# Where split weights begin in on-chip memory, modulo 256 bytes, in a two-block transformer kernel

## The chip, the cores and the metric

One core of a Trainium2 chip. The metric is the device time of one launch, in microseconds (us), the median of several runs. All arithmetic is fp32 to the reader; large products are made of three single-pass products of fp32r operands (below).

## The reference

Two transformer blocks, 256 tokens, width 1024. The first has two layers and carries a context of another 256 tokens beside the tokens, so that its first layer works on 512 columns; its last layer needs of the context only keys and values, and works on 256.

```python
for layer in range(2):
    h_ctx = modulate(rms_norm(ctx, norm_mix[layer]), c_shift1, c_scale1)
    qc, kc, vc, hyc, gc = split(h_ctx @ w_in[layer])        # the last layer: kc, vc only
    h = modulate(rms_norm(x, norm_mix[layer]), shift1, scale1)
    q, k, v, hy, g = split(h @ w_in[layer])
    attn, hyo = latent_attention(q, k, v, kc, vc), hyena_mix(hy, ...)
    merged = g_attn * (attn @ w_o_attn) + g_hyena * (hyo @ w_o_hyena)
    x = x + gate1 * (merged @ w_out[layer])                 # the context likewise, not in the last layer
    x = x + gate2 * swiglu(modulate(...), w_gate_up[layer], w_down[layer])
# second block: a mixer (convolution and dilated attention), memory attention, 32 experts
x = x + mixed(x @ w_in_2) @ w_out_2
x = x + memory_cross_attention(h, m, w_xq, w_xk, w_xv, w_xo)
x = x + hierarchical_moe(h, ...)                            # 32 experts of 1024 x 512, top 2
return rms_norm_2(x, final_norm_g)
```

## The kernel before

**Layout.** Activations lie with the channel on the 128 partitions and tokens along the free axis: tile k of 8 is `[128, tokens]`. A weight matrix is cut into blocks of 128 x 128; eight blocks make a unit of 1024 columns, 4096 bytes in each partition (`UF = 1024`, `UB = 8`). The units come from HBM in one long order (`stream_order`), each with one DMA of 512 KB on SyncE's queue (line 2842), into a ring of `NS = 6` places. A DMA into a place waits until TensorE has used the unit that lay there (`stream.spent`). After the last unit SyncE goes on with the experts' weights (line 2890): 192 transfers of 1024 KB into 15 slots, three of which are the ring and one the high places; the first of them stands right behind the last unit of the ring in SyncE's queue.

**Split weights.** Every streamed weight is split: ScalarE copies the unit, rounded to fp32r, into one of `NHI = 3` high places (`ac_split`, line 431), and VectorE subtracts that from the unit and leaves the low part in the ring place itself (`ve_split`, line 439). Activations are held as a high and a low part too (HH and H, or parts of `area`, KF, VT, YF, KX, VX, tmp). A product is then three: high weight by high activation, high by low, low by high.

**Direct and turned products.** In a direct product the weight block is stationary (it is loaded into the array) and the activations move: `pe_block` (line 460, nearly all), `pe_pair` (line 475), `pe_down` (line 1608) and line 2104. In a turned product 128 tokens are stationary and the weights move: the values of `w_in` (line 927, 256 columns), the values of `w_in_2` (line 1833, 256 columns) and `w_xv_2` (line 1974, 512 columns). The first layer's direct products move 512 columns, and so do the two key blocks of the second layer; all other direct products move 256. TensorE's instructions are in a fixed order; a matmul is preceded by the load of its stationary operand, which runs beside the matmul before it.

**Addresses.** Tiles are allocated one after the other from the address behind a scratch region of 16384 bytes (the default of the builder) and 128 bytes of constants: X begins at 16512, which is 128 modulo 256. X, H, HH, area, KX, VX, VT, YF, KF have sizes that are multiples of 256 bytes, and so all begin at 128 modulo 256; every block within them is a multiple of 512 bytes further on. `con` begins there too; behind it come smaller tiles, tmp and PPT begin at 32 modulo 256. The ring begins at 192064, that is 64 modulo 256, and its places are 4096 bytes apart; the high places begin at 216640, 64 modulo 256 as well. The last of them ends at 228928, and the partition has 229376 bytes.

Lines that the prediction names: 431 and 439 (the splits), 460, 475, 1608 (direct products), 927, 1833, 1974 (turned products), 701 and 709 (the modulation's multiplies and sums, on tiles of the same shape as a unit), 2842 and 2890 (SyncE's transfers).

Of the kernel before, what the change touches and what calls it, by code (L numbers as in the profile page):

```python
# [16 lines left out]
P = 128  # L17
EPS = 1e-6
LN_EPS = 1e-5
UB = 8  # L20
EB = 16
UF, EF = UB * P, EB * P
NS = 6
NHI = 3
# [101 lines left out]
class Signal:  # L126
# [4 lines left out]
    def __init__(self, sem):  # L131
        self.sem, self.n, self.value = sem, 0, {}
# [79 lines left out]
class Stream:  # L212


    def __init__(self, units, slots, sems, ub):
        self.units, self.slots, self.sems, self.ub = units, slots, sems, ub
        self.where = {u: i for i, u in enumerate(units)}
        self.spent = {}

    def slot(self, i):  # L220
        return self.slots[i % len(self.slots)]
# [9 lines left out]

STREAM2 = [("w_xk_2", 0, 6), ("w_in_2", 0, 22), ("w_xv_2", 0, 8), ("w_xk_2", 6, 7), ("w_out_2", 0, 8), ("w_xk_2", 7, 8),
# [8 lines left out]
def stream_order():  # L241
    units = []
    for l in range(2):
        units += [("w_in", l, u) for u in range(24)]
        for j in range(8):
            units += [("w_in", l, 24 + 2 * j), ("w_in", l, 25 + 2 * j), ("w_o_attn", l, j)]
            if j % 2 == 0:
                units.append(("w_o_hyena", l, j // 2))
        for name, n in (("w_out", 8), ("w_gate_up", 44), ("w_down", 22)):
            units += [(name, l, u) for u in range(n)]  # L250
    for name, u0, u1 in STREAM2:
        units += [(name, 0, u) for u in range(u0, u1)]
    return units

# [13 lines left out]
def two_blocks_kernel(nc, T):  # L268
    ctx = ExitStack()
    with ctx:  # L270
# [8 lines left out]
        N = 256  # L279
        X = sb("X", 4096)[:, :].rearrange("p (k t) -> p k t", k=8)  # L280
# [38 lines left out]
        ring, ringr = sb2("ring", NS * UF)  # L319
        his_flat, his = sb2("his", NHI * UF)  # L320
# [48 lines left out]

        def sem(name):  # L370
            return ctx.enter_context(nc.semaphore(name))
# [29 lines left out]
        stream = Stream(stream_order(), [ring[:, i * UF:(i + 1) * UF] for i in range(NS)], [sem(f"s_w{i}") for i in range(NS)], UB)  # L401
# [6 lines left out]
        eslots += [ring[:, i * EF:(i + 1) * EF] for i in range(NS // 2)]  # L408
# [7 lines left out]
        def hi_slot(n):  # L416
            return his[:, (n % NHI) * UF:(n % NHI + 1) * UF]

        def lo_slot(i):
            r = i % NS  # L420
            return ringr[:, r * UF:(r + 1) * UF]
# [451 lines left out]
        pos = {b: n for n, b in enumerate(W_IN_ORDER)}  # L873
# [2163 lines left out]
```

## Time and profile before

| | |
|---|---|
| median of 3 runs | 2082.8 us (2080.1, 2082.8, 2088.5) |
| the profiled execution, first to last instruction | 2084.6 us |
| TensorE matmul / weight load busy | 91% / 75% |
| VectorE / ScalarE / GpSimd busy | 55% / 43% / 1% |
| mean granted TensorE clock | 0.967 of full |

The profiled execution has no time of its own besides its span; the span lies inside the three runs. A clock of 1.00 in a row is 2.4 GHz, 0.50 is 1.2 GHz. Durations of matmuls overlap, since they are pipelined: the pace of a run of matmuls is the distance from start to start, not the duration of one. From 1575 us on the kernel streams the experts' weights at about 420 GB/s to its end.

### The profile page before, as it was taken

The page shows a single profiled execution, that of the slowest core. Times are in us where ns is not written, and L with a number is a line of the kernel's source. Part 1 is how long each engine was busy: PE and PEld are TensorE (multiplying, and loading weights), DVE is VectorE, ACT ScalarE, POOL GpSimd, SP SyncE. Part 2 cuts the span into 40 slices and gives each one's busy share as a digit, 9 for nine tenths or more (in the row PEclk, how much of TensorE's full clock was granted, in tenths as well). Part 3 has the DMA queues.
Part 4 walks back from the last instruction along what each step waited for, and adds up shares of the span by engine and source line. Part 5 has one row for each costly group of instructions (what it writes and reads, how often), then busy time and mean ns, then how long its engine had stood idle before and what let it go on. Part 6 is the DMA issues. An engine that isn't in the chain of part 4 may idle for free.

```text
span 2084.6 us, 33760 instructions
## 1 busy us (share of the span) xinstructions
PE 1889.2 (91%) x14150; PEld 1554.0 (75%) x14150; DVE 1156.6 (55%) x1898; ACT 903.5 (43%) x1532; POOL 16.9 (1%) x31
## 2 busy tenths in 40 slices
PE   7999989999999999999899999999999767776666
PEld 4877668888778888798699999997898544454344
DVE  3555757776887788567656667689755111111012
ACT  4333345665756677455445555634844000000001
POOL 0000000000000000000000000000000000000000
PEclk8999999999999999999999999999999998999987
DMA  8222024553555555234055555543247999999995
GB/s 319 85 71 81 1 76 158 183 179 105 180 179 177 188 193 170 91 102 142 11 182 192 182 183 184 173 162 112 90 144 325 420 420 420 419 419 420 420 421 236
DMA packets 91121, 428.01 MB, mean 205 GB/s; under 512 B 11089, under 2 KB 12754, under 8 KB 66002
## 3 DMA queue, kind: packets, MB, share of 16 engines
q1 hardware_dynamic: 78866, 382.51, 49.3%
q10 hardware_dynamic: 12096, 43.26, 6.2%
q8 instruction: 114, 1.87, 0.4%
q14 instruction: 45, 0.37, 0.1%
HBM read 424.68 MB, written 1.05 MB: 204 GB/s over the span
## 4 chain that ended last, share of the span: by engine, by line
PE 64%; DMA 20%; DVE 8%; ACT 5%; issue 2%; SPq 1%; ACTq 0%; POOL 0%; DVEq 0%; POOLq 0%
PE bank L460 41%; PE bank L1608 8%; DMA area<-in_w 8%; DMA his<-in_w 4%; DMA ring<-in_w 4%; DMA PPT<-in_w 3%; PE bank L475 2%; PE bank L2497 2%; PE bank L2453 1%; DVE st L1259 1%; PE bank L1187 1%; PE bank L2104 1%; PE bank L927 1%; ACT PPT L1204 1%; DVE ring_r L439 1%
## 5 line engine op out<-in xcount | busy, mean ns | idle before, releaser
L439 DVE TENSOR_TENSOR ring_r<-ring,his_r 128x1024 fp32r<-128x1024 f32 x314 | 383.5, 1223 | 226.9 <-ACT his_r L431 225.5
L460 PE MATMUL bank<-HH_r,his_r 128*128 128x256 f32 (+1 forms) x1504 | 499.1, 332 | 1.4 <-DVE ring_r L439 1.4
L460 PE MATMUL bank<-HH_r,ring_r 128*128 128x256 f32 (+1 forms) x1504 | 492.2, 327 | 0.0
L460 PE MATMUL bank<-H_r,his_r 128*128 128x256 f32 (+1 forms) x1440 | 472.8, 328 | 0.0
L431 ACT ACTIVATE his_r<-ring 128x1024 fp32r<-128x1024 f32 x314 | 330.6, 1055 | 303.5 <-PE bank L460 273.4
L460 PEld LDWEIGHTS bank<-HH_r,his_r 128*128 128x128 f32 x1504 | 284.1, 189 | 35.2 <-issue 8.6
L460 PEld LDWEIGHTS bank<-HH_r,ring_r 128*128 128x128 f32 x1504 | 283.7, 189 | 25.1
L460 PEld LDWEIGHTS bank<-H_r,his_r 128*128 128x128 f32 x1440 | 270.7, 188 | 27.0 <-issue 1.0
L2469 DVE TENSOR_TENSOR tmp<-tmp,bank 128x128 f32<-128x128 f32 x64 | 18.4, 288 | 385.9 <-ACT tmp L2462 262.7
L460 PE MATMUL bank<-area_r,his_r 128*128 128x256 f32 (+1 forms) x480 | 148.8, 322 | 0.0
L2453 PE MATMUL bank<-area,KF 128*32 128x128 f32 x1888 | 86.1, 312 | 44.3 <-DMA area<-in_w 39.3
L1608 PE MATMUL bank<-VT_r,ring_r 128*128 128x512 f32 (+1 forms) x352 | 118.6, 337 | 0.0
L1608 PE MATMUL bank<-YF_r,his_r 128*128 128x512 f32 (+1 forms) x352 | 118.1, 336 | 0.0
L1608 PE MATMUL bank<-VT_r,his_r 128*128 128x512 f32 (+1 forms) x352 | 117.5, 334 | 0.0
L2453 PEld LDWEIGHTS bank<-area,KF 128*32 128x32 f32 x1888 | 70.6, 125 | 58.2 <-DMA area<-in_w 49.9
L460 PEld LDWEIGHTS bank<-area_r,his_r 128*128 128x128 f32 x480 | 90.1, 190 | 7.4
L2508 ACT ACTIVATE H<-bank 128x512 f32<-128x512 f32 x16 | 9.6, 597 | 191.3 <-PE bank L2497 191.3
L709 ACT ACTIVATE rst<-rst 128x1024 f32<-128x1024 f32 x80 | 83.6, 1045 | 1.6 <-DVE rst L701 1.6
L2497 PE MATMUL bank<-area,tmp 128*32 128x512 f32 x256 | 56.9, 646 | 20.1 <-DMA area<-in_w 19.5
L1335 ACT ACTIVATE VT_r<-area 128x512 fp32r<-128x512 f32 (+1 forms) x96 | 49.9, 523 | 51.0 <-PE bank L1608 45.3
L1608 PEld LDWEIGHTS bank<-YF_r,his_r 128*128 128x128 f32 x352 | 66.1, 188 | 7.7
L1608 PEld LDWEIGHTS bank<-VT_r,his_r 128*128 128x128 f32 x352 | 65.9, 187 | 7.6 <-DVE YF_r L1339 0.2
(415 smaller groups left out, 3301.0 us busy)
## 6 DMA issues: line engine op xcount, KB each, us to landing
area<-in_w SPq DMA_DIRECT2D x91, 1024.0 KB, 27.3
ring<-in_w_in SPq DMA_DIRECT2D x102, 512.0 KB, 3.5
ring<-in_w_gate_up SPq DMA_DIRECT2D x88, 512.0 KB, 3.5
ring<-in_w SPq DMA_DIRECT2D x36, 1024.0 KB, 27.4
HH<-in_w SPq DMA_DIRECT2D x26, 1024.0 KB, 26.8
ring<-in_w_down SPq DMA_DIRECT2D x44, 512.0 KB, 3.5
KX<-in_w_mod_rows ACTq DMA_DIRECT2D x28, 512.0 KB, 3.5
VX<-in_w_mod_rows ACTq DMA_DIRECT2D x28, 512.0 KB, 3.5
```

The source lines that it names most:

```text
L431: ac.eng.activation(hi_slot(n), stream.slot(u), ACT.Copy).then_inc(*ac_hi.up(n))
L439: ve.eng.tensor_tensor(lo_slot(u), stream.slot(u), hi_slot(n).bitcast(F32), ALU.subtract).then_inc(*ve_lo.up(n))
L460: ins = pe.eng.matmul(out, a, b, start=k == 0 and m == 0, stop=end)
L475: ins = pe.eng.matmul(out, a, b, start=k + m == 0, stop=k == 7 and m == 2)
L709: ac.eng.activation(prod, prod, ACT.Copy, accum_out=MODS[l][:, j, s:s + 1]).then_inc(*ac_mod.up("sum", n, s))
L927: ins = pe.eng.matmul(vb[tb // 2][:, o:o + 256], x[:, k, sl], w, start=k == 0 and n == 0 and o == 0, stop=k == 7 and n == 2 and o > 0)
L1187: ins = pe.eng.matmul(out[:, 0:256], vs(kc), c.pts[g % 2][:, kc * 256:(kc + 1) * 256], start=kc == 0, stop=kc == c.nk - 1)
L1204: ac.eng.activation(p[:, m * w:(m + 1) * w], src[:, m * w:(m + 1) * w], ACT.Exp, bias=st[:, so + m:so + m + 1], scale=c.rq(h, i + m) if c. ...
L1335: ac.eng.activation(hi, src, ACT.Copy).then_inc(*ac_cut.up(*key))
L1608: ins = pe.eng.matmul(banks.ap("ff", l, 4 * half + n)[:, 0:t], w, x, start=k == 0 and i == 0, stop=k == 21 and i == 2)
L2453: ins = pe.eng.matmul(out[32 * n:32 * n + 32, 0:P], HG[g % 2][:, k, 32 * j:32 * j + 32], w, start=k == 0, stop=k == 7, tile_position=(0, 3 ...
L2497: ins = pe.eng.matmul(out[32 * j:32 * j + 32, :], AT[j][:, 32 * k:32 * k + 32], w, start=k == 0, stop=k == 3, tile_position=(0, 32 * j))
```

## The change

Each streamed unit gets a lead, the number of floats by which it begins behind the start of its ring place and of its high place. Places become 64 floats (256 bytes) wider, `UW = UF + 64`. The lead is 0 (`BEHIND_512`), 16 (64 bytes, `BEHIND_256`) or 48 (192 bytes, `BEHIND_TURNED`), by the width of the products that read the unit. The class: the first block's layer 0, the two key units of its layer 1 and `w_xv_2` are 0; the value units of `w_in` and `w_in_2` are 48; everything else is 16. A small tile `level` in front of the ring brings the ring, and with it the high places, to the residue modulo 256 at which X begins. The scratch region is set to 8192 bytes, which makes room. The order of units, of instructions and of waits is the same, and so are all sizes that are moved or computed.

```diff
--- before.py
+++ after.py
@@ -212,13 +212,14 @@
 class Stream:
 
 
-    def __init__(self, units, slots, sems, ub):
+    def __init__(self, units, slots, sems, ub, leads=None):
         self.units, self.slots, self.sems, self.ub = units, slots, sems, ub
+        self.leads = leads or [0] * len(units)
         self.where = {u: i for i, u in enumerate(units)}
         self.spent = {}
 
     def slot(self, i):
-        return self.slots[i % len(self.slots)]
+        return self.slots[i % len(self.slots)][:, self.leads[i]:self.leads[i] + self.ub * P]
 
     def arrived(self, i):
         return self.sems[i % len(self.slots)], 16 * (i // len(self.slots) + 1)
@@ -229,6 +230,9 @@
 
 
 
+FIRST_BLOCK = ("w_in", "w_o_attn", "w_o_hyena", "w_out", "w_gate_up", "w_down")
+UW = UF + 64
+BEHIND_512, BEHIND_256, BEHIND_TURNED = 0, 16, 48
 STREAM2 = [("w_xk_2", 0, 6), ("w_in_2", 0, 22), ("w_xv_2", 0, 8), ("w_xk_2", 6, 7), ("w_out_2", 0, 8), ("w_xk_2", 7, 8),
            ("w_xq_2", 0, 8), ("w_xo_2", 0, 8)]
 
@@ -253,6 +257,18 @@
     return units
 
 
+def stream_leads(units, values):
+    leads = []
+    for name, l, u in units:
+        if name == "w_in" and u in values or name == "w_in_2" and 16 <= u < 22:
+            leads.append(BEHIND_TURNED)
+        elif name in FIRST_BLOCK and l == 0 or name == "w_in" and u < 2 or name == "w_xv_2":
+            leads.append(BEHIND_512)
+        else:
+            leads.append(BEHIND_256)
+    return leads
+
+
 def expert_order():
     units = []
     for g in range(8):
@@ -277,6 +293,7 @@
             return t, nc.alloc_sbuf_tensor_at(name + "_r", [P, cols], F32R, offset=at)
 
         N = 256
+        level = nc.sbuf_base
         X = sb("X", 4096)[:, :].rearrange("p (k t) -> p k t", k=8)
         H, HL = (t[:, :].rearrange("p (k t) -> p k t", k=8) for t in sb2("H", 4096))
         hh_flat, HH = sb2("HH", 4096)
@@ -316,8 +333,9 @@
         PP = [PPS[:, 512 * i:512 * i + 512] for i in range(2)]
         st = sb("st", 64)
         epsc = sb("epsc", 2)
-        ring, ringr = sb2("ring", NS * UF)
-        his_flat, his = sb2("his", NHI * UF)
+        sb("level", (level - nc.sbuf_base) % 256 // 4)
+        ring, ringr = sb2("ring", NS * UW)
+        his_flat, his = sb2("his", NHI * UW)
         psum = [ctx.enter_context(nc.psum_tensor(f"bank{i}", [P, 512], F32)) for i in range(8)]
 
 
@@ -367,6 +385,8 @@
         SG = [KX[:, 0, 256 * i:256 * i + 256].rearrange("p (b s) -> p b s", b=2) for i in range(2)]
         SGT = [VX[:, i, :] for i in range(2)]
 
+        pos = {b: n for n, b in enumerate(W_IN_ORDER)}
+
         def sem(name):
             return ctx.enter_context(nc.semaphore(name))
 
@@ -398,14 +418,15 @@
             return vec[0:rows, VEC[key] + i:VEC[key] + i + n]
 
         ident = cc("ident")
-        stream = Stream(stream_order(), [ring[:, i * UF:(i + 1) * UF] for i in range(NS)], [sem(f"s_w{i}") for i in range(NS)], UB)
+        stream = Stream(stream_order(), [ring[:, i * UW:(i + 1) * UW] for i in range(NS)], [sem(f"s_w{i}") for i in range(NS)], UB,
+                        stream_leads(stream_order(), [pos[b] for b in (10, 11)]))
         where = stream.where
 
         first = Stream([("w_mod", 0, u) for u in range(16)], [area[:, i * UF:(i + 1) * UF] for i in range(11)] +
                        [hh_flat[:, i * UF:(i + 1) * UF] for i in range(4)] + [KX_flat[:, :]], [sem(f"s_m{i}") for i in range(16)], UB)
         eslots = [con[:, 256:256 + EF]] + [area[:, i * EF:(i + 1) * EF] for i in (1, 2, 3, 0, 6, 4, 5)]
         eslots += [PPT[:, :], hh_flat[:, 0:EF], hh_flat[:, EF:2 * EF], his_flat[:, 0:EF]]
-        eslots += [ring[:, i * EF:(i + 1) * EF] for i in range(NS // 2)]
+        eslots += [ring[:, 2 * i * UW:2 * i * UW + EF] for i in range(NS // 2)]
         experts = Stream(expert_order(), eslots, [sem(f"s_e{i}") for i in range(len(eslots))], EB)
         over = Stream([(name, e, u) for e in range(32) for name, u in OVER_ORDER], [rsts_flat[:, :]], [sem("f_w")], UB)
         s_out = sem("s_out")
@@ -414,11 +435,12 @@
         nth = {i: n for n, i in enumerate(cut_units)}
 
         def hi_slot(n):
-            return his[:, (n % NHI) * UF:(n % NHI + 1) * UF]
+            at = n % NHI * UW + stream.leads[cut_units[n]]
+            return his[:, at:at + UF]
 
         def lo_slot(i):
-            r = i % NS
-            return ringr[:, r * UF:(r + 1) * UF]
+            at = i % NS * UW + stream.leads[i]
+            return ringr[:, at:at + UF]
 
 
         def ac_split(ac, upto):
@@ -870,7 +892,6 @@
 
 
 
-        pos = {b: n for n, b in enumerate(W_IN_ORDER)}
 
         def tokens(l):
             return 256 if l else 512
@@ -3026,7 +3047,7 @@
         arrays[name] = tiles(I[name][0], ub=EB)
     arrays["w2_2"] = rows_outermost(I["w2_2"][0])
 
-    nc = _bacc.Bacc("TRN2", target_bir_lowering=False, num_devices=1)
+    nc = _bacc.Bacc("TRN2", target_bir_lowering=False, num_devices=1, dynamic_dma_scratch_size=8192)
     T = {n: nc.dram_tensor("in_" + n, a.shape, mybir.dt.from_np(a.dtype), kind="ExternalInput").ap() for n, a in arrays.items()}
     T["out"] = nc.dram_tensor("out_0", (P, 8, 256), F32, kind="ExternalOutput").ap()
     T["deep"] = ("w_in", "w_gate_up", "w_mod", "w_mod_rows", "w_o_attn", "w_o_hyena", "w_out", "w_down", "w1_2", "w3_2", "w2_2")
```

## Rows read from the trace of the kernel before

**Rows 1.** The page: busy TensorE, and the chain's shares by engine and line

```profile
PE 1889.2 (91%) x14150; PEld 1554.0 (75%) x14150; DVE 1156.6 (55%) x1898; ACT 903.5 (43%) x1532; POOL 16.9 (1%) x31
...
PE 64%; DMA 20%; DVE 8%; ACT 5%; issue 2%; SPq 1%; ACTq 0%; POOL 0%; DVEq 0%; POOLq 0%
PE bank L460 41%; PE bank L1608 8%; DMA area<-in_w 8%; DMA his<-in_w 4%; DMA ring<-in_w 4%; DMA PPT<-in_w 3%; PE bank L475 2%; PE bank L2497 2%; PE bank L2453 1%; DVE st L1259 1%; PE bank L1187 1%; PE bank L2104 1%; PE bank L927 1%; ACT PPT L1204 1%; DVE ring_r L439 1%
```

**Rows 2.** Chain in order of time: start us, us, engine, tile, line, count

```profile
626.04 131.85 PE bank L460 x576
...
901.47 11.00 PE bank L927 x96
...
1150.08 68.08 PE bank L460 x576
...
1270.38 56.80 PE bank L1608 x480
...
1411.58 5.67 PE bank L1833 x48
...
1465.16 2.80 PE bank L1974 x12
```

**Rows 3.** Windows of TensorE: from:to, length, busy (count), clock, DMA share, GB/s

```profile
120.20:122.20 2.00, 2.00 (x6) 0.50 0.05 16
1341.00:1345.00 4.00, 4.00 (x23) 0.55 0.00 0
53.00:62.00 9.00, 9.00 (x82) 1.00 0.27 95
640.00:740.00 100.00, 100.00 (x439) 1.00 0.57 189
1160.00:1210.00 50.00, 50.00 (x427) 1.00 0.57 189
```

**Rows 4.** Timeline at half clock: start us, us, engine, line, tiles, array, columns

```profile
120.09 0.63 PE L460 MATMUL bank<-H_r,his_r 128*128 128x512 f32 x1
...
121.79 0.63 PE L460 MATMUL bank<-HH_r,ring_r 128*128 128x512 f32 x1
...
1340.61 0.41 PE L460 MATMUL bank<-HH_r,ring_r 128*128 128x256 f32 x1
...
1341.89 0.41 PE L460 MATMUL bank<-HH_r,ring_r 128*128 128x256 f32 x1
```

**Rows 5.** Groups by line: count | busy us, mean ns | idle before, releaser

```profile
L439 DVE TENSOR_TENSOR ring_r<-ring,his_r 128x1024 fp32r<-128x1024 f32 x314 | 383.5, 1223 | 226.9 <-ACT his_r L431 225.5
L701 DVE TENSOR_TENSOR rst<-KX,PPT 128x1024 f32<-128x1024 f32 x28 | 34.1, 1219 | 0.0
L431 ACT ACTIVATE his_r<-ring 128x1024 fp32r<-128x1024 f32 x314 | 330.6, 1055 | 303.5 <-PE bank L460 273.4 <-PE bank L2104 8.2 <-PE bank L927 7.3
L709 ACT ACTIVATE KX<-KX 128x1024 f32<-128x1024 f32 x28 | 29.3, 1046 | 0.0
```

**Rows 6.** The page: GB/s by slice, DMA queues, issues with KB and us to landing

```profile
GB/s 319 85 71 81 1 76 158 183 179 105 180 179 177 188 193 170 91 102 142 11 182 192 182 183 184 173 162 112 90 144 325 420 420 420 419 419 420 420 421 236
...
q1 hardware_dynamic: 78866, 382.51, 49.3%
q10 hardware_dynamic: 12096, 43.26, 6.2%
q8 instruction: 114, 1.87, 0.4%
...
area<-in_w SPq DMA_DIRECT2D x91, 1024.0 KB, 27.3
...
ring<-in_w SPq DMA_DIRECT2D x36, 1024.0 KB, 27.4
```

**Rows 7.** Timeline of SyncE's queue where the experts' transfers begin

```profile
1572.21 3.15 SPq L2842 DMA_DIRECT2D ring<-in_w_xo  x2
1575.41 0.43 SPq L2890 DMA_DIRECT2D con<-in_w  x1
```

## The prediction

> **What bounds the kernel now.** I read the page first: TensorE is busy 91% of the span, and the chain that ended last lies on it for 64%; line 460 alone carries 41% of the span, lines 1608 and 475 another 8% and 2% [rows 1]. All three are the same thing: a product of split weights (high by high, high by low, low by high), in single-pass fp32r. Next I read that chain in order of time, for its long unbroken runs. They show the pace: with 512 columns moving, 131.85 us for 576 products is 228.9 ns each; with 256 columns, 68.08 for 576 is 118.2 and 56.80 for 480 is 118.3 [rows 2]. The windows view sharpens it: a stretch holds (its length plus one product's duration) divided by the pace. So 100.00 us with 439 products of 0.39 us is 228.7 ns, and 50.00 us with 427 of 0.28 us is 117.7 [rows 3]. I use 228.9 and 117.7. In these stretches the granted clock is 1.00, TensorE never idles, and no wait ends late. What would make such a stretch shorter is a faster product, nothing else.
>
> How fast could it be? Where the granted clock was 0.50 (1.2 GHz), the same products start 4 intervals in 1.70 us (425 ns, 512 columns) and 6 intervals in 1.28 us (213 ns, 256 columns) [rows 3, 4]: the columns and nothing beside them. At 2.4 GHz that would be 213 and 107 ns. So at full clock a product loses 16 ns with 512 columns and 11 ns with 256, though no engine waits. The rows don't name the cause. The one thing that runs beside a product is the load of the next stationary operand, and both read the same partitions of on-chip memory.
>
> One pair of groups speaks for a matter of addresses. Line 927 has the operands turned round (256 columns of weights move, activations are stationary): 82 products of 0.28 us touch 9.00 us, or 113.2 ns [rows 3], and 96 with their slow start take 11.00 us (114.6) [rows 2]. Same columns, same fp32r, same clock, 4.5 ns less. What I vary in thought is the distance modulo 256 bytes from where the running product's moving operand begins to where the next stationary operand begins. By the order of allocation activations begin at 128 and ring and high places at 64. So direct products have distance 192, turned ones 64. But line 1833, turned as well and with distance 64, needs 118.1 (5.67 us for 48) [rows 2]: the same distance shows both paces.
>
> **The change, part by part.** No instruction, semaphore wait or DMA is added, removed or reordered on any queue; addresses alone move. The ring moves to residue 128 by 64 bytes of padding, each place is 256 bytes wider, and a unit begins 0, 64 or 192 bytes into it.
>
> (1) *Direct products, 256 columns.* Distance 192 becomes 64. Their count, from the streams: layer 1 has 36 + 8 + 4 + 8 + 44 + 22 = 122 units, the second block 48, each 24 products, 4080 in all. The nearest rows are line 927's 113.2 (a gain of 4.5 ns) and line 1833's 118.1 (no gain). I take 113.2: it held over 192 products in two layers, in long runs like those of the direct products, where line 1833 is broken up by waits. The last 144 products (6 units) come after the expert transfers have begun, which is the part where nothing is gained (below): 3936 x 4.5 = 17.7 us.
>
> (2) *Direct products, 512 columns.* Distance 192 becomes 0, which no fp32r row here has. Count: 124 units of layer 0 and the two key units of layer 1, x 24 = 3024. Bounds: 213 ns below (a gain of 16); above, the worst pace of any relation here, line 1974's 233.3 (2.80 us for 12, distance 64) [rows 2], a loss of 4.4. Between ends so far apart I go by the 256-column case: there the better placement keeps (113.2 - 106.5) / (117.7 - 106.5) = 0.6 of the loss. The same share of 16 ns is 9.5, so 222.5 ns, a gain of 6.4: 3024 x 6.4 = 19.4 us. This is the weakest term.
>
> (3) *Turned products.* Lines 927 and 1833 keep distance 64: nothing. Line 1974 (96 products) goes from 64 to 0: at most 0.02 us each, inside attention where VectorE sets the end. Nothing.
>
> (4) *The splits.* ScalarE and VectorE read and write ring and high places at one common residue before and after. VectorE's split takes 1223 ns, and a multiply of the same shape whose operands lie at other residues 1219; ScalarE 1055 against 1046 [rows 5]. Bounds +-4 and +-9 ns on 314 units. They are hidden: a unit lasts 24 x 118 = 2.8 us on TensorE against 1.22 on VectorE. If products drop to 113 it lasts 2.7, still covered. Zero.
>
> (5) *DMA.* A ring place is written from residues 128, 192 or 64 instead of 64. In the transfer-bound tail a megabyte lands in 27.4 us in the ring (residue 64) and 27.3 in the area (128) [rows 6]. Zero. The scratch cut from 16 to 8 KB pays for the 2304 wider bytes; its users would be GpSimd's transfers, and the queues shown are the two hardware ones and instruction fetch [rows 6]. Zero.
>
> **From the sum to the span.** Not every product is on the chain. Lines 460, 1608 and 475 make 51.4% of 2084.6 us there, 1071 us; their products at the paces above come to 3024 x 0.2289 + (4080 - 192) x 0.1177 = 1150 us (192 are line 2104's). Share 0.93. So (17.7 + 19.4) x 0.93 = 34.5 us. The tail: the first expert transfer is issued at 1575.41, right behind the last ring units (their wait is for TensorE to free a place) [rows 7]; from there 192 MB-sized transfers (201 MB) at the 420 GB/s of the page [rows 6] need 479 us, and TensorE waits for them. The tail keeps its length and moves forward with its start. What is late next is again a product: no new wait arises. The profiled span of 2084.6 lies inside the three runs (median 2082.8), so I subtract from the median: 2048 us.
>
> **The rule against it.** Rows first: at full clock a product costs 228.9 and 117.7 ns, 16 and 11 above its columns, and 113.2 at line 927 [rows 2, 3]. The Trainium skill, page SBUF — State Buffer, section "Who interferes with whom", says that TensorE has two independent read ports, one for the moving and one for the stationary operand, and never waits on anyone. By that the placement is worth nothing and the sum is 2083, rival 3. The difference between line 927 and line 460 is what the rule doesn't explain. The page TensorE: Matmul & The Clock Gate, section "Back-to-back issue gap", gives N / 2.4 + 2.5 ns, 215.8 for 512 columns; by it, an estimate, rival 1 ends near 2029 instead of 2022.
>
> **Rivals.**
> 1. *Free of loss at 512.* The 0 distance removes all 16 ns: 3024 x 15.9 = 48, with (1) 65.8 x 0.93 = 61, 2022 us. For: nothing but the cold rows. Against: the best pair at 256 kept 60% of its loss.
> 2. *One width gains alone.* Direct products settle as line 1833 does, or distance 0 is no better than 192: 17.7 x 0.93 = 16 or 19.4 x 0.93 = 18 us, 2065 to 2066. For: line 1833 has the new distance and the old pace.
> 3. *It doesn't do what it says.* The loss hangs on the order of reads, the output bank or the start of a run, not on residues; 927's gain is its four alternating outputs. 2083 us. For: 927 and 1833.
> 4. *Slower.* Distance 0 makes load and stream meet more often; 512 columns run at line 1974's 233.3 and 256 gains nothing: 3024 x 4.4 x 0.93 = +12, 2095 us. For: with 512 columns distance 64 is worse than 192, and 0 lies between the two. With (1) in full it decides only from 235 ns up.
>
> **How the numbers follow.** Chances: forecast (512 between 218 and 227 ns, 256 near 113) 0.45; rival 1 0.12; rival 2 0.20; rival 3 0.14; rival 4 0.09. The forecast's own range: 512 at 218 to 227 gives 2035 to 2061. The full range must take in rivals 2 and 3 to reach 8 in 10: 2030 to 2084; it leaves out rival 4 and most of rival 1. A measurement of this kernel can tell about 0.5%, 10.4 us, from no change. Faster by more (below 2072.4): 0.45 + 0.12 + 0.20 = 0.77; within: 0.14; slower: 0.09.
>
> **What would show it.** After: 576 products at line 460 with 512 columns in about 128 us of chain instead of 131.85, 576 with 256 columns in about 65.3 instead of 68.08; line 927 still 11.00 and line 1833 5.67; split durations unchanged; first expert transfer near 1541 instead of 1575.41, tail 489 us as now. Wrong if the 512 runs hold over 227 ns, if 256 columns run at 118, or if a wait for VectorE's low parts grows beyond a few us.

## The result, and the profile after

| | before | after |
|---|---|---|
| time, median of 4 runs each | 2082.9 us | 2071.5 us |
| ratio, 95% interval | | 0.9934, 0.9919 to 0.9949 |
| profiled execution: span | 2084.6 us | 2069.7 us |
| TensorE busy | 1889.2 us | 1880.4 us |
| first expert transfer issued at | 1575.4 us | 1562.4 us |

The change makes the kernel 0.66% faster, 13.7 us by the ratio (11.4 between the medians). The forecast was 34.5 us: right in sign, too large by a factor of 2.5. 2071.5 lies inside the full range (2030 to 2084), but outside the 2035 to 2061 that the forecast's own mechanism was given. A second set of runs gave 0.9934 again (0.9920 to 0.9947).

The page of the changed kernel: busy TensorE, and the chain's shares. Line numbers have moved: 460 is now 482, 1608 is 1629, 927 is 948, 1833 is 1854, 1974 is 1995, 439 and 431 are 461 and 453, 2890 is 2911.

```profile
PE 1880.4 (91%) x14150; PEld 1547.8 (75%) x14150; DVE 1155.6 (56%) x1898; ACT 903.6 (44%) x1532; POOL 17.0 (1%) x31
...
PE bank L482 42%; DMA area<-in_w 8%; PE bank L1629 8%; DMA his<-in_w 4%; DMA ring<-in_w 4%; DMA PPT<-in_w 3%; PE bank L497 2%; PE bank L2518 2%; PE bank L2474 1%; DVE st L1280 1%; PE bank L1208 1%; ACT PPT L1225 1%; PE bank L948 1%; DVE ring_r L461 1%; PE bank L2125 1%
```

The bound is what it was [rows 1]: TensorE on the products of split weights. The chain in order of time, to hold against [rows 2] (start us, us, engine, tile, line, count):

```profile
52.91 11.41 PE bank L948 x96
...
625.01 130.57 PE bank L482 x576
...
897.96 11.01 PE bank L948 x96
...
938.33 34.05 PE bank L482 x288
...
1144.28 65.29 PE bank L482 x576
...
1399.68 5.67 PE bank L1854 x48
```

576 products of 512 columns take 130.57 us for 131.85, or 226.7 ns each for 228.9. 576 of 256 columns take 65.29 for 68.08, or 113.3 for 118.2. But 288 products of 256 columns, the same line and the same distance, take 34.05 us, 118.2 each: they gained nothing. The turned products of line 948 take 11.41 us in layer 0 and 11.01 in layer 1, those of line 1854 5.67 as before. Line 927 had taken 11.00 in both layers. The windows say the same, against [rows 3]: 442 products in 100 us for 439, 445 in 50 us for 427.

```profile
640.00:740.00 100.00, 100.00 (x442) 1.00 0.59 195
1160.00:1210.00 50.00, 50.00 (x445) 1.00 0.58 194
```

The splits and the transfers are unmoved, against [rows 5] and [rows 6]; SyncE's queue reaches the experts 13.0 us earlier, against [rows 7]:

```profile
L461 DVE TENSOR_TENSOR ring_r<-ring,his_r 128x1024 fp32r<-128x1024 f32 x314 | 383.3, 1223 | 220.9 <-ACT his_r L453 219.6
L453 ACT ACTIVATE his_r<-ring 128x1024 fp32r<-128x1024 f32 x314 | 330.8, 1056 | 292.8 <-PE bank L482 262.6 <-PE bank L2125 7.9 <-PE bank L948 7.5
...
area<-in_w SPq DMA_DIRECT2D x91, 1024.0 KB, 27.5
...
ring<-in_w SPq DMA_DIRECT2D x36, 1024.0 KB, 27.3
...
1562.44 0.43 SPq L2911 DMA_DIRECT2D con<-in_w  x1
```

### The profile page after: what moved, and what is told of

Same layout as the page of the kernel before. It is cut to its first block, busy times and chain, and to the rows that moved or that the text cites. A ratio compares the mean times of both kernels' runs of the same rounds, so it can differ in the third digit from the quotient of the medians.

```text
span 2069.7 us, 33760 instructions
## 1 busy us (share of the span) xinstructions
PE 1880.4 (91%) x14150; PEld 1547.8 (75%) x14150; DVE 1155.6 (56%) x1898; ACT 903.6 (44%) x1532; POOL 17.0 (1%) x31
## 4 chain that ended last, share of the span: by engine, by line
PE 65%; DMA 19%; DVE 8%; ACT 5%; issue 2%; SPq 1%; ACTq 0%; DVEq 0%
PE bank L482 42%; DMA area<-in_w 8%; PE bank L1629 8%; DMA his<-in_w 4%; DMA ring<-in_w 4%; DMA PPT<-in_w 3%; PE bank L497 2%; PE bank L2518 2%; PE bank L2474 1%; DVE st L1280 1%; PE bank L1208 1%; ACT PPT L1225 1%; PE bank L948 1%; DVE ring_r L461 1%; PE bank L2125 1%
## 5 line engine op out<-in xcount | busy, mean ns | idle before, releaser
L1629 PEld LDWEIGHTS bank<-VT_r,ring_r 128*128 128x128 f32 x352 | 66.1, 188 | 6.9
```

The source lines that it names most:

```text
L1629: ins = pe.eng.matmul(banks.ap("ff", l, 4 * half + n)[:, 0:t], w, x, start=k == 0 and i == 0, stop=k == 21 and i == 2)
```

## How the runs are compared

In what follows "distance" is as in the prediction: start of the next stationary operand less start of the running moving operand, modulo 256 bytes. "Pace" is the mean interval from the start of one direct product to the start of the next, from all records of a trace; intervals over 240 ns (512 columns) or 124 ns (256), which hold a wait or are the slow first ones of a run, are left out. "Settled" means the mean of the last intervals of a piece, once they repeat. A "lead" is in floats of 4 bytes. "By pace" is 3024 times the change of the first pace plus 4080 times that of the second. All kernels on this table compute the reference in full.

| kernel | distances 512 / 256 | pace 512 | pace 256 | by pace | ratio to before (95%) | as us |
|---|---|---|---|---|---|---|
| before | 192 / 192 | 229.06 | 117.76 | | | |
| changed | 0 / 64 | 227.05 | 114.69 | -18.6 | 0.9934 (0.9919 to 0.9949) | -13.7 |
| changed, again | 0 / 64 | 227.09 | 114.47 | -19.4 | 0.9934 (0.9920 to 0.9947) | -13.7 |
| only_512 | 0 / 192 | 227.08 | 117.71 | -6.2 | 0.9964 (0.9950 to 0.9977) | -7.5 |
| only_256 | 192 / 64 | 229.03 | 115.11 | -10.9 | 0.9956 (0.9943 to 0.9969) | -9.2 |
| all_48 | 192 / 192 | 229.02 | 117.59 | -0.8 | 1.0001 (0.9992 to 1.0011) | 0.2 |
| alternate | 0 / 64 and 192 | 227.07 | 114.34 | -20.0 | 0.9929 (0.9909 to 0.9950) | -14.8 |
| fine | 252 / 76 | 233.19 | 113.75 | -3.9 | 0.9989 (0.9978 to 1.0000) | -2.3 |
| best | 0 / 76 | 227.08 | 113.78 | -22.2 | 0.9899 (0.9881 to 0.9917) | -21.0 |
| sure | 120 / 76 | 226.86 | 113.77 | -22.9 | 0.9916 (0.9901 to 0.9931) | -17.5 |
| swapped | 64 / 0 | 233.32 | 119.83 | +21.3 | 1.0081 (1.0063 to 1.0099) | +16.9 |

Over the ten kernels the time follows the column "by pace" with a factor of 0.8 (least squares through zero), in both directions.

## Experiments: which part of the change carries the gain

The leads are one line of the kernel. Each of these three is the changed kernel with other numbers there:

```diff
-BEHIND_512, BEHIND_256, BEHIND_TURNED = 0, 16, 48
+BEHIND_512, BEHIND_256, BEHIND_TURNED = 0, 48, 48     # only_512
+BEHIND_512, BEHIND_256, BEHIND_TURNED = 48, 16, 48    # only_256
+BEHIND_512, BEHIND_256, BEHIND_TURNED = 48, 48, 48    # all_48
```

**only_512.**

> Only the products of 512 columns get their new distance (0); those of 256 columns stay at distance 192. Theory A (the traces of before and after): 512 columns at 226.7 ns for 228.9, 256 columns at 117.8 everywhere, so 5 to 6 us under the kernel before (ratio 0.997, about 2077). Rival, from the forecast: the wide products carry most (19 us at full size), about 2065. Rival C: the whole gain comes from the narrow products, 2083.

Measured: 2077.9 us, ratio 0.9964, paces 227.08 and 117.71. Near what the theory said (5 to 6 us less; measured 7.5, interval 4.8 to 10.4). The forecast's 19 us for this width is out, and so is rival C.

**only_256.**

> Only the products of 256 columns get their new distance (64); those of 512 stay at distance 192. Theory A: 512 columns at 228.9 ns as before; 256 columns at 113.3 in part of the runs and 117.8 in the rest, so 8 to 12 us under the kernel before (about 2073), and with only_512 the two gains add up to that of the changed kernel. Which runs are at which pace may differ from the changed kernel, since they begin at other moments. Rival C: the full gain of 11 to 14 us.

Measured: 2076.0 us, ratio 0.9956, paces 229.03 and 115.11. The two gains (7.5 and 9.2 us) add up to 16.7, the changed kernel's 13.7 within the intervals. This run's own interval (6.5 to 11.9 us) touches rival C's 11 to 14; it is only_512 that rules rival C out.

**all_48.**

> The changed kernel with a lead of 48 columns in every place: wider places, ring at the activations' residue and the smaller descriptor memory stay, but every distance is that of the kernel before (192 and 64). Theory A: same time as before (ratio 0.998 to 1.002), products at 117.8 and 228.9 ns. Theory B (spacing of the places or the smaller descriptor memory brings part of the gain): 4 us or more under the kernel before.

Measured: 2084.5 us, ratio 1.0001. Padding, wider places and the smaller scratch are worth nothing to within 0.1%; the gain is that of the distances.

The rows of the chain put the four side by side. Of only_512, then of only_256, then of all_48 (512 columns, then 256):

```profile
625.12 130.57 PE bank L482 x576
...
1147.57 67.84 PE bank L482 x576
```

```profile
627.64 131.85 PE bank L482 x576
...
943.88 32.78 PE bank L482 x288
...
1147.71 68.08 PE bank L482 x576
```

```profile
626.22 131.85 PE bank L482 x576
...
1150.65 68.08 PE bank L482 x576
```

In only_256 it is the 288 products that run fast (32.78 us, 113.8 each) and the 576 that run slow (68.08, 118.2): the other way round than in the changed kernel, at the same addresses. In the second trace of the changed kernel the 288 were fast as well:

```profile
938.75 32.78 PE bank L482 x288
```

So at distance 64 there are two paces, and neither the program nor the addresses say which one a run takes.

## Experiments: the products alone

**sweep.** A kernel that holds nothing but triples of products, one segment of 60 (256 columns) or 36 (512) after another. Every operand lies where it is told; between segments TensorE waits for one copy on VectorE. Its heart:

```python
for i in range(n // 3):
    k, at = i % 8, 512 * (i % 8)
    ...
    for m in range(3):
        c = P * ((k + (m == 2)) % 8)
        a = 512 * ((k + (m == 1)) % 8)
        ins = pe.matmul(out, w[:, c:c + P], xs[:, a:a + width], start=k == 0 and m == 0, ...)
```

> A kernel of its own: it leaves the whole of the reference out and runs only fp32r products on TensorE, in the triples of the kernel (stationary and moving operands alternate between two blocks), one segment after another: widths 256 and 512, the distance (start of the next stationary operand less start of the running moving operand, modulo 256 bytes) from 0 to 240 in steps of 16 bytes, twice each after breaks of two lengths; then 256 columns at distances 64, 0 and 16 after eight lengths of break; the same distances from other starting residues; and a run with no break in which the distance jumps. Theory A (the pace is set by the distance, and at 256 columns and distance 64 by how the run began as well): distance 192 gives 117.8 ns at 256 columns and 228.9 at 512, distance 64 gives 113.3 or 117.8 from segment to segment at 256, distance 0 gives 226.7 at 512; a segment with the same distance and other residues gives the same. Theory B (the pace comes from the ring, the banks or the residue itself, not from the distance): the segments of one width all show one pace, or pieces with one distance and other residues differ by 2 ns or more. Theory C (the distance decides alone): all eleven restarts at distance 64 show 113.3.

Its chain of waits has one row for each segment. 256 columns at distances 0, 64 and 192; 512 columns at 0, 64 and 192; and last 256 columns at 64 once more, after another length of break:

```profile
54.63 7.46 PE bank L111 x60
...
85.25 7.10 PE bank L111 x60
...
146.42 7.35 PE bank L111 x60
...
299.90 8.47 PE bank L111 x36
...
335.43 8.68 PE bank L111 x36
...
406.82 8.53 PE bank L111 x36
...
631.20 7.36 PE bank L111 x60
```

Settled paces (from the starts of the products): 120.0, 113.3 and 117.8 ns; 226.7, 233.3 and 228.9. With no transfer and no other engine at work the kernel's own paces come back to a tenth of a nanosecond, so they are TensorE's alone. Theory B fell: every distance tried from several starting residues settled at the same pace or pair of paces. Theory C fell too: of 13 starts at distance 64, 9 ran at 113.3 and 4 at 117.8 (the last row above is one: 7.36 us for 7.10). No distance in steps of 16 bytes is better than 113.3 or 226.7, and 512 columns at distance 0 need some products to settle, here five: 337, 236, 228, 233, 231, then 226, 227 ns. In other starts it was from one to eleven.

**starts.** The same kernel with other segments; what is new is that one segment follows another with no break.

```diff
+    for first in (192, 160, 224, 128, 240):
+        for n in (3, 6, 12, 24):
+            for pause in (32, 80, 144, 176):
+                out.append((256, first, first, 128, n, pause))
+                out.append((256, 64, 64, 128, 36, 0))
```

> A kernel of its own again: it leaves the reference out and runs only fp32r products in triples. It asks when the products of 256 columns at distance 64 take the pace of 113.3 ns. After each of four lengths of break, 3, 6, 12 or 24 products at another distance (192, 160, 224, 128 or 240) come first and 36 at distance 64 follow without a break; then six pieces of 24 that alternate between distance 192 and 64; then, without a break, all distances up and down in steps of 16 bytes at 256 and at 512 columns. Theory A (there are two paces, the one that is running holds, and a change of distance can switch it): after 192 or 160 the pieces at 64 run at 113.3 ns after every break (from breaks alone it was 9 of 13), and after a piece at 64 in the fast pace distance 192 holds 113.3 too, so that the alternating pieces run at 113.3 from the second on. Rival (the switch seen in the sweep was one chance start): the pieces at 64 are fast in about two of three whatever comes before them, and 192 always returns to 117.8. At 512 columns theory A says 226.7 at distances 0 and 240 and 228.9 to 234.5 elsewhere, in both directions.

The 36 products at distance 64 ran fast in 15 of 16 cases behind products at 192, 160 or 224, in 16 of 16 behind 240, in 10 of 16 behind 128. Four times six pieces of 24 alternated between 192 and 64. Two of these four, and one of four pieces of 48 products at 192 alone:

```profile
536.22 16.72 PE bank L120 x144
553.22 16.71 PE bank L120 x144
...
604.26 5.94 PE bank L120 x48
```

144 products in 16.72 us are 116.1 each with the slow first one; the first 24 (distance 192) ran at 117.8, all the rest at 113.3, the later pieces at distance 192 among them. Alone, 48 products at 192 take 5.94 us, 117.8 once settled. So the running pace holds across a change of distance, and 192 has the fast pace too, if something brings it there. The rival of chance starts fell for these; behind 128, 10 of 16 is no more than breaks alone gave. At 512 columns one point of the expectation fell: distance 16, which had settled at 233.3 after breaks, held 226.7 when the products came to it from 0.

**alternate.**

```diff
-            leads.append(BEHIND_256)
+            leads.append(48 if len(leads) % 2 else BEHIND_256)
```

> The changed kernel, with the 256-column units in turn at distance 64 and 192 in place of 64 for all. Theory A (192 to 64 switches to the fast pace, which then holds at both distances): long runs at 113.3 ns nearly everywhere, also in the two stretches where the changed kernel ran at 117.8 (909 to 977 and 1353 to 1366 us); 256-column products on average 113.5 to 114.3 ns, 2 to 5 us under the changed kernel (2067 to 2070 where it has 2071.5). Rival (the distance alone decides, half the units are lost): 256-column products at 116, 5 us over the changed kernel.

Measured: 2069.7 us, ratio 0.9929, pace 114.34. The rival (116) fell, with half the units back at the distance of the kernel before. The pace is at the weak end of what was expected (113.5 to 114.3) and the time can't be told from the changed kernel's. Every stretch of 71 products and more was fast, the 288 too; but of the short ones, of 24 or so, some 17 ran at 117.8, as many as in the changed kernel.

**mixed and full.** The two stationary operands of a triple at different distances, and all distances in steps of 4 bytes.

```diff
+        for d in range(0, 256, 32):
+            for e in range(0, 256, 32):
+                if d != e:
+                    out.append((width, d, e, 128, n, 32))          # mixed
...
+    for d in range(0, 256, 4):
+        for pause in (32, 112, 176):
+            out.append((256, d, d, 128, 36, pause))                # full
```

> A kernel of its own: it leaves the reference out and runs only fp32r products in triples. First the two stationary operands of a triple stand at different distances (the first two reads at one, the third at another, all pairs in steps of 32 bytes), at 256 and 512 columns; then steps of 4 bytes around distance 64 at 256 columns, and around 0 at 512. Theory A (each operand's reads interfere by their own distance): a mixed triple lies between the paces of its two distances, 113 to 120 ns and 226.7 to 235 ns, and a few bytes off 64 or 0 the good pace is kept or lost in one step. Rival (only the residue in coarse lines of 32 or 64 bytes counts): steps of 4 bytes change nothing within a line. A pair below 113.3 or 226.7 ns would be a better layout than the changed kernel's.

> A kernel of its own: it leaves the reference out and runs only fp32r products in triples, at all distances from 0 to 252 in steps of 4 bytes, 256 columns after three lengths of break and 512 columns after two. Theory A' (from the steps of 4 bytes around 64: 52, 64, 76 and 88 gave 113.3, those between 117.8 to 120): the good distances stand in rows 12 bytes apart, so more of them lie further on, and 113.3 and 226.7 ns are the lowest paces anywhere. Theory A (only multiples of 64 bytes are special): outside 52 to 88 nothing reaches 113.3, and 252 and 0 are the only ones at 226.7. At 76 bytes the fast pace is to stand from the second product on after all three breaks, at 64 only after some products or not at all.

A mixed triple is not a mean of its parts: two reads at 64 and the third at 192 gave 113.3, the other way round 118.9, and two at 64 with the third at 0 or 96 gave 122.2, above either. At 512 columns no mixed triple was faster than 228.9. These are one start each. The rival of coarse lines fell: around 64 a step of 4 bytes changes the pace (60: 119, 68: 118.3). In steps of 4 bytes most distances ran between 115.5 and 122 ns. The fast pace of 256 columns showed at 52 and 76 in three starts of three, at 64 and 88 in two, at 180 in one; 226.7 at 512 columns in both starts at 0, 120, 132, 156 and 252, in one at 100 and 240. The fast distances at 256 columns stand 12 bytes apart from 52 to 88, but the series doesn't go on, so both theories of the expectation for full fell. Nothing was faster than 113.3 and 226.7. The row of full for distance 76 beside those of 72 and 80, one start each:

```profile
325.70 4.54 PE bank L108 x36
...
335.22 4.37 PE bank L108 x36
...
344.58 4.55 PE bank L108 x36
```

My expectation said that 76 would be fast from the second product on; it got there in all three starts, but after three, seven and nine products.

## Experiments: a finer choice, and why one half of it failed

**fine and the changed kernel beside it.**

```diff
-BEHIND_512, BEHIND_256, BEHIND_TURNED = 0, 16, 48
+BEHIND_512, BEHIND_256, BEHIND_TURNED, BEHIND_VALUES = 63, 19, 45, 1
```

`BEHIND_VALUES` is the lead of `w_xv_2`, which two added lines take out of the first class (so line 482 is 484 here, 948 is 950).

> The changed kernel with distances at which the products alone took the fast pace at once: 76 bytes for 256 columns (lead of 19 columns), 252 for 512 (lead 63), turned ones at 76 and 252 (leads 45 and 1). Theory A' (the fast pace is reached from any start at 76): 256-column products at 113.3 to 113.7 ns everywhere, line 948 at 113.3 in both layers, 512-column ones at 226.7 with fewer slow products after each break; 5 to 8 us under the changed kernel, about 2065 (ratio to the kernel before 0.990). Rival 1 (in the kernel the spread of waits and the other operands disturb as much as before): within 2 us of the changed kernel. Rival 2 (places that begin at odd multiples of 4 bytes make their transfers or the splits slower): transfer of a place to landing over 29 us or the split over 1223 ns, and a time over the changed kernel's.

> The changed kernel once more, on the same chip as the finer distances, so that the two stand beside each other: 0.992 to 0.995 of the kernel before. If the slow stretches of 256 columns (909 to 977 us, 1353 to 1366 us) come from how each run happens to begin, they may lie elsewhere in this trace; if they are fixed by the program, they lie at the same products.

Measured: fine 2082.0 us, ratio 0.9989; the changed kernel on the same chip 2071.0, 0.9934. The miss has one place. 256 columns did as hoped (first row below: 576 in 65.29 us; the 288 in 32.78). The 512 ones ran at 233.3:

```profile
85.73 5.65 PE bank L484 x24
92.17 5.71 PE bank L484 x24
...
633.72 134.40 PE bank L484 x576
...
955.31 32.78 PE bank L484 x288
...
1158.53 65.29 PE bank L484 x576
```

134.40 us for 576 are 233.3 each. The first two rows are the key: 24 products of 512 columns in 5.65 us settled at 226.7, 24 in 5.71 at 233.3, at one distance. Three such stretches, of 24 products each, took the fast pace; all the others ran at 233.3. So distance 252 too has two paces. Alone it had shown 226.7 in one start of mixed and two of full, three in all (the expectation for breaks says four), and that was too few. Rival 2 (odd addresses slow the transfers or the splits) is out: the units of `w_in` and `w_gate_up` land in 3.5 us as before, and the split takes 1224 ns. (The megabyte transfers of the experts go to ring places without a lead and can't speak for it. The units of `w_down` took 4.3 us for 3.5; they took 4.2 in best and 3.5 in sure, which share their distance in layer 1.) The turned products of 256 columns ran at 120.1 ns at distance 76, where the changed kernel's, at 64, had 115.7: what is good for direct ones is not for them. In the second trace of the changed kernel line 948 of layer 1 took 11.41 us, where the first has 11.01, which again is the same program at another pace. Of the two slow stretches that the expectation names, the short runs up to 938 us were slow in both traces, all but one; the 288 products behind them and the stretch of 1353 to 1366 us were fast in the second.

**breaks.** 24 lengths of break for each distance.

```diff
+    for width, d, n in ((256, 64, 24), (256, 76, 24), (256, 52, 24), (256, 192, 24), (512, 0, 18), (512, 252, 18), (512, 120, 18)):
+        for pause in range(8, 8 + 24 * 20, 20):
+            out.append((width, d, d, 128, n, pause))
```

> A kernel of its own: it leaves the reference out and runs only fp32r products in triples, after 24 lengths of break for each of seven settings: 256 columns at distances 64, 76, 52 and 192, 512 columns at 0, 252 and 120. Theory A'' (each distance has more than one steady pace, and how the run begins picks one): 64 at 113.3 in some two of three, 192 in none, 76 and 52 in nearly all; 0 at 226.7 in nearly all; 252, which took 226.7 in all four starts alone and 233.3 in 28 of 31 in the kernel, shows both paces over 24 starts. Rival (something in the kernel that these products lack, transfers or the other engines, makes 252 slow there): 252 at 226.7 in 24 of 24.

| columns, distance | settled at the fast pace | the others |
|---|---|---|
| 256, 64 | 15 of 24 | 117.8 |
| 256, 76 | 24 of 24 | |
| 256, 52 | 18 of 24 | 117.7 to 120.0 |
| 256, 192 | 2 of 24 | 117.8 |
| 512, 0 | 24 of 24, after five to eleven products | |
| 512, 252 | 5 of 24 | 233.3 |
| 512, 120 | 24 of 24, after one to four products | |

Seven rows of its chain: two starts at 256 columns and distance 64, two at 76, and three at 512 columns and 252:

```profile
59.10 3.11 PE bank L105 x24
62.48 3.02 PE bank L105 x24
...
150.91 3.00 PE bank L105 x24
154.21 3.02 PE bank L105 x24
...
512.45 4.47 PE bank L105 x18
517.20 4.37 PE bank L105 x18
521.87 4.49 PE bank L105 x18
```

The rival (something in the kernel that the products alone lack) fell: 252 is slow in 19 of 24 starts with nothing beside it. Two points of the expectation missed: 192, said to be fast in none, was fast in two, and 52, said to be fast in nearly all, in 18. Distance gives the paces that are possible, and the start picks one.

**best and swapped.**

```diff
+BEHIND_512, BEHIND_256, BEHIND_TURNED = 0, 19, 48     # best
+BEHIND_512, BEHIND_256, BEHIND_TURNED = 16, 0, 48     # swapped
```

> The changed kernel with one number changed: the direct products of 256 columns at distance 76 (lead 19) in place of 64; 512 columns stay at 0 and turned ones at 64. Theory A: 256-column direct products at 113.7 ns on average, as in the kernel with the finer distances (114.5 to 114.7 in the changed kernel), 512-column ones at 227.1, so 3 to 4 us under the changed kernel: about 2068, ratio to the kernel before 0.992. Rival (the shorter products are eaten by waits for the splits): within 1 us of the changed kernel, 0.9934.

> The changed kernel with the two distances interchanged: 512 columns at 64, 256 columns at 0. Theory A (the products alone showed 233.3 and 120.0 ns there): 3024 products at plus 4.3 ns and 4080 at plus 2.2 ns against the kernel before are 13 + 9 = 22 us, of which the share on the chain of waits makes it slower than the kernel before by 15 to 22 us, about 2101 (ratio 1.007 to 1.011). Rival B (it is the wider places or the lead as such that helps): no slower than the kernel before.

Measured: best 2066.0 us, ratio 0.9899 (0.9881 to 0.9917), where 2068 and 0.992 were expected; its rival (waits eat the gain) fell. It is the lowest of all, and its interval ends just below the changed kernel's (0.9919 and 0.9920 at the low end of its two sets); the pace is 113.78 for 114.69. Swapped 2104.1 us, 1.0081, where 2101 was expected: paces found on products alone foretold a loss in the kernel to 3 us. Swapped's rival B (wider places or the lead as such help) fell. The chain of best, then of swapped:

```profile
623.62 130.57 PE bank L482 x576
...
936.82 32.78 PE bank L482 x288
...
1140.94 65.55 PE bank L482 x576
```

```profile
633.65 134.40 PE bank L482 x576
...
955.52 34.67 PE bank L482 x288
...
1165.99 69.27 PE bank L482 x576
```

Swapped shows one thing more. Where its granted clock was 0.50, its products start 4 intervals in 1.71 us (427 ns, 512 columns, distance 64) and 6 in 1.28 us (213 ns, 256 columns, distance 0). The kernel before had the same at distance 192 [rows 4], and so have the changed kernel at 0 and 64 and fine at 252 and 76. At half clock the distance made no difference.

```profile
122.50 0.63 PE L482 MATMUL bank<-HH_r,his_r 128*128 128x512 f32 x1
...
124.21 0.63 PE L482 MATMUL bank<-H_r,his_r 128*128 128x512 f32 x1
...
1358.14 0.41 PE L482 MATMUL bank<-HH_r,ring_r 128*128 128x256 f32 x1
...
1359.42 0.41 PE L482 MATMUL bank<-HH_r,ring_r 128*128 128x256 f32 x1
```

**sure.** As best, with the direct products of 512 columns at distance 120:

```diff
+BEHIND_512, BEHIND_256, BEHIND_TURNED, BEHIND_VALUES = 30, 19, 48, 0
```

> As the kernel with 256 columns at distance 76, and now the direct products of 512 columns at 120 (lead 30) in place of 0: alone they took 226.7 ns after 24 of 24 breaks and settled sooner (18 products in 4.36 us for 4.39). Theory A'' (what counts is how many starts find the fast pace when the products run alone): 512-column products at 226.7 ns in every start in the kernel, 697 us or 1 to 3 us less in all, 256 columns as before at 113.8, time within 0.15% of 2066.0 and no worse. Rival (an address that is no multiple of 64 bytes fails in the kernel, as 252 did): many starts at 233, 12 us more, about 2078.

Measured: 2067.6 us, ratio 0.9916 (0.9901 to 0.9931), pace 226.86, and every stretch of 512 columns at the fast one; the rival (2078) fell. The share of fast starts alone did foretell the kernel, for 120 as for 252. The further gain of 1 to 3 us did not show; best and sure can't be told apart.

## Why the prediction was right or wrong

**What bounds the kernel:** right. The long runs on TensorE were the place, and distances alone moved their pace. That the load of the next operand and the stream of the running one get in each other's way, as the prediction supposed, is not shown: the runs show that their distance counts, not how.

**Term 1, 256 columns (17.7 us forecast; 12.5 by pace, 9.2 us measured alone):** mechanism right, size off. The step that failed is the choice between two rows that contradicted each other: "I take 113.2: it held over 192 products in two layers". Both rows were true, since line 927's 113.2 and line 1833's 118.1 at one distance [rows 2] are the two paces that distance 64 has. The reason given for the slow one, that waits break line 1833 up, was half of it: a wait gives a new start, and 9 of 24 starts at 64 take the slow pace and keep it. The 288 products at 938 us are such a run, long and unbroken. Weighted 15 to 9, the term is 3936 x 4.5 x 0.63 = 11 us. The 15 and 9 came later, but the trace of before, with its two rows, called for a weight.

**Term 2, 512 columns (19.4 us forecast; 6.1 by pace, 7.5 measured alone):** the largest miss, 13 us of the sum. The failed step is "the same share of 16 ns": the share of the loss that one width keeps doesn't carry over to the other. Distance 0 gives 226.7, and over all 64 distances nothing in the sweeps went below that; the 222.5 of the sum doesn't exist. Of the trace's rows, the only one for another distance at 512 columns was line 1974's 233.3, 4.4 ns above 228.9. A gain of like size, 4 ns at most or 13 us, was all that a row spoke for; measured were 2.0 ns.

**Term 3, turned products:** nothing, as forecast. They ran at 115.2 and 115.7 ns before and after, though single stretches changed pace (line 948 in layer 0 took 11.41 us).

**Terms 4 and 5, splits and DMA:** zero, as forecast; all_48 shows it in one number, 1.0001.

**From the sum to the span:** 0.93 forecast, 0.8 measured over ten kernels, 2.4 us of the changed kernel's sum. In its trace the 18.6 us by pace are some 16.5 us once all intervals between direct products are counted in, those with waits too, and the span is 14.9 us shorter; where the rest went was not traced. Expert transfers began 13.0 us earlier. The tail kept its length, 509.2 us before and 507.3 after, from there to the end of the span. (The 489 us named for it among the signs was not the number that the rows give.)

**Range and signs.** The forecast's mechanism was given 2035 to 2061 us, and 2071.5 lies outside it, near rival 2's 2066. That the full range holds it is luck: it was drawn wide for rivals 2 and 3, and both fell. Of the named signs, the 512-column run took 130.57 us and not 128, and the experts began at 1562 and not 1541; the 256-column run of 576 took its 65.3. The two signs of failure came true in part: 512 columns ran at 226.7 settled, just under the 227 named, and one run of 288 at 256 columns ran at 118.

**Rivals.** Rival 1 fell: at full clock no placement comes to 213 ns, half of the interval at half clock, nor to the 215.8 of its second estimate; the best is 226.7. Rival 2 fell, both widths gain. Rival 3 fell: products alone, with every other engine idle, ran between 113.3 and 122 ns by address. The Trainium skill, page SBUF — State Buffer, section "Who interferes with whom", gives TensorE two independent read ports and no waits, by which the placement would be worth nothing; the measured paces don't agree, and they decide. Of rival 4 the slower paces are real, but at other distances: 512 columns ran at 233.3 at distance 64, not at 0, and swapped is the kernel that is slower by them.

## What to carry to other kernels

Where a trace shows one form of instruction at two paces with nothing waiting, both belong in the sum, with a share for each; look for what a run's start decides before calling one row the rule. For long chains of fp32r products on TensorE, the start addresses of stationary and moving operands are worth trying: the paces at distances 0, 64 and 192 lie up to 3% apart at 512 columns and 6% at 256. Measure the candidates alone, from some twenty different starts each, and take the one that is fast from all of them, not the one that was fast four times.

## What the runs showed of the hardware

- The pace of fp32r products of 128 x 128 at a granted clock of 1.00 depends on the distance of the operands' addresses: 113.3 to 122.2 ns at 256 columns, 226.7 to some 238 at 512 (full), with no other engine at work. At half clock the products ran at 213 and 427 ns at every distance that a kernel here had (192, 0, 64, 252 and 76), with no such loss.
- Several distances have more than one steady pace (64 and 192: 113.3 and 117.8; 252 at 512 columns: 226.7 and 233.3). A run picks one at its start, keeps it for hundreds of products (576 in one row of the chain), and can carry it across a change of distance: from 64 to 192 at 256 columns and from 0 to 16 at 512, but not from 0 to 192 at 512, where it was 228.9 again (starts). Four bytes decide between good and bad.
- The steady intervals repeat: 113, 113, 114 and 226, 227, 227 at the fast paces; 226, 229 and 232 in turn, now and then 231, at distance 192 with 512 columns; 117, 118 and 119 with a mean of 117.8 at 256.
- What in a start picks the pace is open. The length of the break does change it, but it isn't all: 512 columns at 252 were fast after a break of 48 columns in mixed and slow after the same in breaks. Why 226.7 and 113.3 are the floor at full clock, 13 and 7 ns above half of the half-clock pace, wasn't settled either.
- All blocks of an operand lie at multiples of 512 bytes from each other, so these runs can't tell whether it is the next stationary operand or the one in use whose distance counts.
